# Expert blocks of mixed width in a mixture-of-experts step: 34 blocks a pass in place of 40, every block's rows placed by a 0/1 product

## The chip, the cores and the metric

One core of a Trainium2 chip runs the kernel alone. The time is device microseconds (us) of one execution, the median of the runs taken. Engines are named as in the profile: PE multiplies matrices, DVE is VectorE, ACT is ScalarE, POOL is GpSimd, SP issues most DMAs. The inputs are fixed; all of them are float32.

## What is computed

One inference step for 128 context tokens and 256 latent tokens of width 1024: adaLN modulation, a mixer (neighbourhood attention beside a gated recurrence), a mixture of experts (MoE), a final RMSNorm. The change is in the MoE, for all 384 tokens `t`:

```
s = sigmoid(t @ w_router); sb = s + b_router
# 8 groups of 8 experts: the 4 groups with the best top-2 sum stay; among them the top 8 experts of sb
wk = s[idx] / sum(s[idx]) * 2.5
gates = zeros(n, 64) with wk at idx
act = silu(t @ w_gate_e) * (t @ w_up_e) * gates        # per expert, width 256
routed = act @ w_down_e ; shared = (silu(t @ w_gate_s) * (t @ w_up_s)) @ w_down_s
x += gate_ffn * (routed + shared)
```

Each token uses 8 of 64 experts: 3,072 pairs of token and expert. An expert's weights are three matrices of 1024 KB: gate and up (together "gu") and down ("dn").

## The kernel before

The first third of the execution computes the mixer. Then the router's choice is turned into tables: experts are sorted by load, and each gets a place in a sequence of **blocks** of 128 rows. A block of kind H holds up to 128 tokens of one expert; a block of kind L holds up to 64 tokens of one expert in rows 0 to 63 and up to 64 of another in rows 64 to 127. Blocks come in 4 groups of 16 experts and 10 blocks (4 H and 6 L): `ORDER0, ORDER = "HHHHLLLLLL", "HLLHLHLLHL"`, so a pass over all experts has 40 blocks. If an expert has more tokens than its places hold, a further pass over all groups follows; with these inputs there is none. The first group is written out, the two in the middle are a loop, the last is written out again. Which experts the first four H blocks use is fixed, so that their weights can be loaded before the routing is known.

For one block at turn `u` PE does, in this order (`block_turn` of PE): `gate_up(u)` (the weights of gate and up stream against the block's tokens; for an L block the two experts use two column tiles of 64 and run side by side), `turn_tokens(u+1)` (transposes of the next block's gathered tokens), `down(u-1)`, two transposes of the activation, `block_rows(u+3)` (a small product that yields token numbers and gates of a later block), and where the block before is *placed*, `place(u-1)`.

A block's output rows reach their tokens in one of two ways. **Scattered**: ACT evicts them, scaled by their gates, into `y_sb`, and POOL adds them to a buffer in HBM (`y_dram`, zeroed earlier) with an indirect DMA that accumulates (`scatter`). **Placed**: ACT writes a rounded high part, DVE the rest (`place_low`), DVE makes a 0/1 matrix from the token numbers (`place_matrix`), PE multiplies the two by it (12 products into six banks, `place`), and DVE adds the six banks to `ffn_acc` in SBUF (`place_sums`). 17 blocks are placed (the last two of them in `place_ending`), 23 scattered. At the end `y_dram` is read back (six loads of 512 KB on SP), added, and everything is gated into `x_sb`.

Weights live in a ring of 5 slots, each with a gu and a dn buffer. SP issues, in program order and with waits, for turn `u` the gu loads of block `u` as soon as `gate_up` has released the slot, and behind them the dn loads of block `u-1`. The gather of a block's tokens (`xg <- h2_dram`, indirect DMA on POOL) is issued two blocks ahead. DVE does per turn: `act_sb`, half of the token copy, the placing work, `a_t`, `numbers` (reductions to `slot_val`, `slot_gate`, `slot_tok`, `slot_row`), `select` (the one-hot for the block four ahead), in turns 2 to 7 of the first group `later_passes` (copies of the tables for further passes, made whether they are needed or not), the shared expert's sums in turns 5 to 7, and last `place_sums`. PE's next `gate_up` waits for the first of these sums, for that frees its bank. The shared expert's down product runs inside turns 5 to 7 of the first group, and the product that spreads `gate_ffn` over the partitions (`spread`, L1189) in turn 4.

Of the kernel before, what the change touches and what calls it, by code (L numbers as in the profile page):

```python
# [13 lines left out]
P = 128  # L14
# [20 lines left out]
ORDER0, ORDER = "HHHHLLLLLL", "HLLHLHLLHL"  # L35
NGRP, EPG, BPG = 4, 16, 10
NPASS_BLK = NGRP * BPG
MAXPASS = 4
# [3 lines left out]
NBLK = NPASS_BLK * MAXPASS  # L42
NSIDE = 2 * NPASS_BLK
FIXED = 4
PLACED = (0, 2, 4, 5, 7)
SCATTERED = BPG - len(PLACED)
FIRST_PLACED = (BPG - 3, BPG - 2)
ENDING = (0, 2, BPG - 3, BPG - 2, BPG - 1)
HEAVY = 16
EMPTY = 1024  # L50
MARK = 4096.0
TABLES = 3 + 7
RC = 387
LAT0 = 131
NTAB = NBLK + 4
# [11 lines left out]
def hybrid_step(nc, x_prompt, x_sample, cache_k, cache_v, state_f, state_b, c, c_ctx,  # L67
# [5 lines left out]
    with ctx:  # L73
        KB = 1024
        arena = ctx.enter_context(nc.sbuf_tensor("arena", [P, 207 * 256 + 160], F32))
# [124 lines left out]
        shared_dn = at("shared_dn", [P, 2048], EX + 48)  # L200
# [4 lines left out]
        shared_sb = at("shared_sb", [P, D], EX + 56)  # L205
        x_t = at("x_t", [P, KD * CAP], EX + 108)
        zeros = at("zeros", [P, D], EX + 108)
        a_sh = at("a_sh", [P, TT, 2 * CAP], EX + 112)
        y_sb = [at(f"y_sb{i}", [P, D], EX + 116 + 4 * i) for i in range(2)]
# [31 lines left out]
        shift = little("shift", [P, 2, NSIDE])  # L241
        row_off = little("row_off", [P, 1])
        slot_row = little("slot_row", [P, UN], I32)
# [13 lines left out]
        seq_rank = little("seq_rank", [NE, NE])  # L257
        side_pick = little("side_pick", [NE, NSIDE])
        seq_pick = little("seq_pick", [NE, NE])
        inv_cap = little("inv_cap", [P, NSIDE])  # L260
        fill = little("fill", [P, NSIDE])
        place[0] = EX + 162.5
        limit[0] = EX + 163.5
        seq_expert = little("seq_expert", [1, MAXPASS * NE], I32)


        ffn = [at(f"ffn{t}", [P, D], EX + 4 * t) for t in range(TT)]
        ffn_b = [at(f"ffn_b{t}", [P, D], EX + 12 + 4 * t) for t in range(TT)]
# [3 lines left out]
        y_r = [at(f"y_r{i}", [P, D], EX + 116 + 4 * i, F32R) for i in range(2)]  # L272
        y_hi = [y_r[0], at("y_hi", [P, D], EX + 36, F32R)]
        y_lo_end = at("y_lo_end", [P, D], 12, F32R)
        y_lo = [at(f"y_lo{i}", [P, D], EX + 44 - 4 * i, F32R) for i in range(2)]
# [5 lines left out]

        y_dram = nc.dram_tensor("y_dram", (2 * NTOK, D), F32, kind="Internal").ap()

# [30 lines left out]
        for n, (kind, i) in enumerate(chunks):  # L314
# [3 lines left out]
        S = {n: sem(n) for n in """added cond_loaded vec_loaded cache_loaded bias_loaded block_loaded  # L318
# [10 lines left out]
            gates_made sides_mm sides_evac picks_made sorted_mm gu_used dn_used b_zero  # L329
            sh_mm sh_silu sh_act sh_at_mm sh_at shd_mm shd_evac shared_loaded early_mm  # L330
# [25 lines left out]
        def experts_of(order):  # L356

            n, blocks = 0, []
            for kind in order:
                blocks.append(tuple(range(n, n + 1 + (kind == "L"))))  # L360
                n += len(blocks[-1])
            assert n == EPG
            return blocks
# [3 lines left out]
        def shared_turn(u, first):  # L367

            return (u - FIRST_SHARED,) if first and FIRST_SHARED <= u < FIRST_SHARED + TT else ()

        def shared_outs(u):

            return bank[2 + (u + 1) % 2], bank[2 + u % 2]

        FIRST_SHARED = 5
        SHARED_BANK = (2, 3, 5)
        SPREAD_TURN = 4
# [5 lines left out]

        first_half = (("router_loaded", 16), ("shared_loaded", 48), ("bias_loaded", 32))

        def heavy_places(order):
            return [x[0] for x, kind in zip(experts_of(order), order) if kind == "H"]

        FIRST_FOUR = heavy_places(ORDER0)


        SLOT0 = [x % RING for x in range(EPG)]
        heavy_slot, light_slots = 3, (1, 2, 4, 0)
        SLOT, lights = [], 0
        for x in range(EPG):
            if x in heavy_places(ORDER):
                SLOT.append(heavy_slot)
            else:
                SLOT.append(light_slots[lights % 4])
                lights += 1  # L400
# [20 lines left out]
        assert not {SLOT[x] for x in turns[False][-1]} & {1, 2}  # L421
        assert [SLOT0[x] for x in turns[False][-1]] == [SLOT[x] for x in turns[False][-1]]

        assert max(PLACED) < UN - 2

        assert {SLOT[x] for x in turns[False][UN - 3]} == {1, 2}
        assert not {SLOT[x] for u in (UN - 2, UN - 1) for x in turns[False][u]} & {1, 2}

        def placed_in(last):
            return ENDING if last else PLACED  # L430

        def is_placed(u, first, last=False):
            return u in FIRST_PLACED if first else u % UN in placed_in(last and u >= 0)

        def first_scatters(u):

            return 16 * sum(v not in FIRST_PLACED for v in range(u))

        def scatters_ahead(b, u, last=False):

            back = 1 if u < 0 else 0
            here = placed_in(last and not back)
            return b * (16 * SCATTERED) + 16 * (len(PLACED) - len(FIRST_PLACED) - SCATTERED * back + sum(v not in here for v in range(u % UN)))

        def places_ahead(b, v, each, last=False, first=False):

            if first:
                return each * FIRST_PLACED.index(v)
# [371 lines left out]
        def _(act):  # L820
# [241 lines left out]
            def shared_out(t, outs):  # L1062
                if t:
                    act.wait_ge(S["x2_ready"], t)
# [1220 lines left out]
```

## Time and profile before

| | us |
|---|---|
| median of 3 runs | 927.61 |
| lowest, highest | 926.42, 934.16 |
| span of the profiled execution | 925.6 |

The profile is of one execution. Its span is from the first to the last instruction. Busy time of PE is modelled at the ends of pipelined matmuls, so the distance from the start of one group of matmuls to the next says more than the busy share. `L1538` is line 1538 of the kernel. A matmul in float32 shows as two instructions. "DMA share" is the busy share of the core's 16 DMA engines.

### The profile page before, as it was taken

How to read it: one execution, taken by the hardware profiler on the slowest of the kernel's cores; microseconds unless marked ns; L12 is line 12 of the kernel's file. 1: busy time of each engine (PE TensorE's matmuls, PEld its weight loads, DVE VectorE, ACT ScalarE, POOL GpSimd, SP SyncE). 2: the span in 40 equal slices, each digit the busy share in tenths (PEclk: the TensorE clock that was granted, in tenths of full speed). 3: DMA queues.
4: the chain of work that ended last, by engine and by line, in shares of the span. 5: the costliest groups of instructions: out<-in, count | busy, mean ns of one | idle time of the engine just before them, and what ended most of it. 6: DMA issues, size and time to landing. Idle time of an engine off the chain costs nothing.

```text
span 925.6 us, 12174 instructions
## 1 busy us (share of the span) xinstructions
PE 876.7 (95%) x4185; PEld 513.0 (55%) x4185; DVE 436.2 (47%) x961; ACT 254.9 (28%) x417; POOL 138.6 (15%) x224
## 2 busy tenths in 40 slices
PE   4799999999999899999999999999999999999991
PEld 2387876899998765443344444444444444444440
DVE  1562493677666554233253442542344442433386
ACT  2536634444423431212211122122112112212211
POOL 7410000000002131122110111011111012012202
PEclk9799999999999999999999999999999999999996
DMA  9974885722237398899999999999999999999971
GB/s 353 350 266 172 302 292 211 159 92 65 79 131 267 138 417 310 271 348 406 379 404 420 404 401 402 421 391 406 409 408 409 421 394 408 411 407 400 404 319 68
DMA packets 82416, 294.24 MB, mean 318 GB/s; under 512 B 16876, under 2 KB 33320, under 8 KB 57408
## 3 DMA queue, kind: packets, MB, share of 16 engines
q1 hardware_dynamic: 62352, 263.21, 71.7%
q0 software_dynamic: 11312, 25.85, 9.4%
q10 hardware_dynamic: 8704, 4.54, 1.9%
q8 instruction: 30, 0.49, 0.2%
q14 instruction: 18, 0.15, 0.0%
HBM read 286.11 MB, written 20.71 MB: 332 GB/s over the span
## 4 chain that ended last, share of the span: by engine, by line
PE 75%; DMA 14%; DVE 4%; issue 3%; ACT 1%; SPq 0%; ACTq 0%; POOL 0%; DVEq 0%; POOLq 0%
PE bank L1538 26%; PE bank L1557 13%; PE bank L1150 8%; PE bank L1152 7%; PE bank L1151 7%; DMA y_dram<-y_sb,slot_row 5%; PE bank L1526 4%; DMA chunk_raw<-in_w_ada_dram 3%; DMA b_t<-in_b_ada_dram 2%; PE bank L1178 1%; DMA h_dram<-h_row 1%; DMA dn<-in_w_down_e_dram 1%; PE bank L1230 1%; PE bank L1452 1%; DMA xg<-h_dram,slot_tok 1%
## 5 line engine op out<-in xcount | busy, mean ns | idle before, releaser
L1538 PE MATMUL bank<-gu,x_t 128*64 128x512 f32 (+1 forms) x1024 | 283.8, 596 | 2.6 <-DVE ffn_acc L2247 1.8
L1538 PEld LDWEIGHTS bank<-gu,x_t 128*64 128x64 f32 (+1 forms) x1024 | 101.3, 150 | 160.7 <-issue 157.4
L1557 PE MATMUL bank<-dn,a_t 128*64 128x512 f32 (+1 forms) x512 | 145.4, 597 | 0.6 <-DMA dn<-in_w_down_e_dram 0.6
L2113 DVE TENSOR_TENSOR act_sb<-silu_sb,bank 128x256 f32<-128x256 f32 x40 | 16.8, 421 | 194.8 <-ACT silu_sb L1111 194.8
L1111 ACT ACTIVATE silu_sb<-bank 128x256 f32<-128x256 f32 x40 | 15.4, 385 | 316.1 <-PE bank L1538 316.1
L1557 PEld LDWEIGHTS bank<-dn,a_t 128*64 128x64 f32 (+1 forms) x512 | 48.5, 150 | 69.8 <-issue 68.8
L1150 PE MATMUL bank<-h_hi,chunk_lo 128*128 128x384 f32 x240 | 84.2, 351 | 0.0
L1152 PE MATMUL bank<-h_hi,chunk_hi 128*128 128x384 f32 x240 | 80.6, 336 | 0.0
L1151 PE MATMUL bank<-h_lo,chunk_hi 128*128 128x384 f32 x240 | 80.4, 335 | 0.0
L792 POOL DMA_INDIRECT y_dram<-y_sb,slot_row x23 | 38.5, 1674 | 259.7 <-DVE slot_row L1996 225.7
L780 POOL DMA_INDIRECT xg<-h_dram,slot_tok x40 | 41.5, 1037 | 197.5 <-DVE slot_row L1996 175.5
L475 DVE TENSOR_TENSOR chunk_lo<-chunk_raw,chunk_hi 128x2048 fp32r<-128x2048 f32 x25 | 57.1, 2287 | 15.8 <-ACT chunk_hi L469 15.7
L469 ACT ACTIVATE chunk_hi<-chunk_raw 128x2048 fp32r<-128x2048 f32 x25 | 47.7, 1914 | 42.5 <-PE bank L1152 42.3
L2129 DVE COPY a_t<-bank 128x256 f32<-128x256 f32 x40 | 16.9, 423 | 76.8 <-PE bank L1666 76.6
L1526 PEld LDWEIGHTS bank<-ident,xg 128*128 128x128 f32 x320 | 35.5, 140 | 27.3 <-issue 26.6
L1150 PEld LDWEIGHTS bank<-h_hi,chunk_lo 128*128 128x128 f32 x240 | 45.0, 188 | 7.1 <-issue 5.4
L2247 DVE TENSOR_TENSOR ffn_acc<-ffn_acc,bank 128x512 f32<-128x512 f32 x78 | 47.8, 683 | 0.4
L1576 PE MATMUL bank<-y_r,place_r 128*128 128x512 f32 x174 | 45.1, 401 | 1.2 <-DVE a_t L2129 1.1
L1094 ACT ACTIVATE y_sb<-bank,slot_gate 128x512 f32<-128x512 f32 x46 | 31.6, 687 | 51.9 <-PE bank L1557 50.6
L1151 PEld LDWEIGHTS bank<-h_lo,chunk_hi 128*128 128x128 f32 x240 | 45.1, 188 | 0.3
L1152 PEld LDWEIGHTS bank<-h_hi,chunk_hi 128*128 128x128 f32 x240 | 45.1, 188 | 0.0
L1526 PE MATMUL bank<-ident,xg 128*128 128x128 f32 x320 | 42.8, 277 | 0.6 <-DMA xg<-h_dram,slot_tok 0.6
(366 smaller groups left out, 1099.9 us busy)
## 6 DMA issues: line engine op xcount, KB each, us to landing
gu<-in_w_gate_e_dram SPq DMA_DIRECT2D x64, 1024.0 KB, 14.7
gu<-in_w_up_e_dram SPq DMA_DIRECT2D x64, 1024.0 KB, 18.1
dn<-in_w_down_e_dram SPq DMA_DIRECT2D x64, 1024.0 KB, 19.5
chunk_raw<-in_w_ada_dram SPq DMA_DIRECT2D x24, 1024.0 KB, 8.8
chunk_raw<-in_w_in_dram SPq DMA_DIRECT2D x18, 1024.0 KB, 5.4
chunk_raw<-in_w_out_dram SPq DMA_DIRECT2D x4, 1024.0 KB, 5.1
y_dram<-zeros POOLq DMA_DIRECT2D x1, 3072.0 KB, 18.6
chunk_raw<-in_w_pa_dram SPq DMA_DIRECT2D x2, 1024.0 KB, 5.1
```

Source lines behind the costliest of these rows:

```text
L469: act.activation(chunk_hi[j % HIGHS][:, :], chunk_raw[slot[n]][:, :], ACT.Copy).then_inc(S["chunk_high"], 1)
L475: dve.tensor_tensor(chunk_lo[slot[n]][:, :], chunk_raw[slot[n]][:, :], chunk_hi[j % HIGHS][:, :].bitcast(F32), ALU.subtract).then_inc(S["c ...
L780: pool.indirect_dma_start(xg[u % 2][:, :], None, h2_dram[:, :], bass.IndirectOffsetOnAxis(ap=slot_tok[:, u % UN:u % UN + 1], axis=0), boun ...
L792: pool.indirect_dma_start(y_dram[:, :], bass.IndirectOffsetOnAxis(ap=slot_row[:, u % UN:u % UN + 1], axis=0), y_sb[u % 2][:, :], None, bou ...
L1150: pe.matmul(out, left[1], right[0], start=start, stop=False)
L1151: pe.matmul(out, left[0], right[1], start=False, stop=False)
L1152: return pe.matmul(out, left[0], right[0], start=False, stop=stop)
L1526: mm = pe.transpose(bank[k // 4][:, (k % 4) * P:(k % 4 + 1) * P], xg[u % 2][:, k * P:(k + 1) * P], ident[:, :])
L1538: mm = pe.matmul(bank[2 + u % 2][at_x, :].rearrange("p (g n) -> p g n", g=2), x_t[:, cols], wide[:, :, k, :], start=(k == 0), stop=(k == K ...
L1557: mm = pe.matmul(outs[half][at_x, :], a_t[:, cols], dn[slot_of(x, first)][:, wc], start=(k == 0), stop=(k == 1))
L1576: return pe.matmul(out[:, :], place_r[:, t * P:(t + 1) * P], y[:, halves[half]], start=start, stop=not start)
L2247: dve.tensor_tensor(ffn_acc[t][:, cols], ffn_acc[t][:, cols], out[:, :], ALU.add).then_inc(S["place_out"], 1)
```

## The change

- A third kind of block, **M**: 96 rows of one expert and 32 of another. PE's tiles are then four column tiles of 32 (`tiles_of`): three with the same weights and one with the other expert's, so 4 matmuls for each k in place of 2 (L) or 1 (H).
- The first group has the blocks "MMMHHLHLHL" (10), the three others "MLLMLLML" (8): 34 blocks. Per pass 12 experts may have up to 96 tokens, 12 up to 32, 4 up to 128, 36 up to 64.
- Nothing is scattered. `y_dram`, its zeroing, `slot_row`, and the loads at the end are gone; `place` follows every block. `y_hi` and `y_lo` are single buffers. At the last turn DVE gates `ffn_acc` into `x_sb` (`sums_in`, six operations) ahead of its other work.
- The shared expert's down product runs before block 0 and starts `ffn_acc` by an ACT copy; its weights come with its gate and up weights, ahead of the MoE. `spread` moves to turn 0.
- Three experts, not four, are loaded before the routing is known; `passes_ready` comes earlier. Slot 4 of the ring holds the shared weights first, also for its dn buffer.
- `later_passes` keeps its place in DVE's turn (turns 2 to 8 of the first group); it has fewer small copies. `select` for an M block is two operations. Tables are made for up to 5 passes, not 4.

The diff, cut to its core:

```diff
-ORDER0, ORDER = "HHHHLLLLLL", "HLLHLHLLHL"
-NGRP, EPG, BPG = 4, 16, 10
+WIDE, NARROW = 96, 32
+ORDER0, ORDER = "MMMHHLHLHL", "MLLMLLML"
+NGRP, EPG, BPG0, BPG = 4, 16, len(ORDER0), len(ORDER)
...
+        def tiles_of(x, u, first):
+            if kind_of(u, first) == "H":
+                return [slice(0, P)]
+            second = x != turns[first][u][0]
+            if kind_of(u, first) == "L":
+                return [slice(HALF * second, HALF * second + HALF)]
+            return [slice(q * QW, q * QW + QW) for q in ((3,) if second else (0, 1, 2))]
...
+        SLOT0 = [(0, 3, 1, 4, 2)[x % RING] for x in range(EPG)]
+        often, others = 1, (3, 4, 2, 0)
+        SLOT = [often if x % 4 == 0 else others[(x - x // 4 - 1) % 4] for x in range(EPG)]
...
-            pool.dma_start(y_dram.rearrange("(t p) d -> p t d", p=P), zeros[:, :].unsqueeze(1).to_broadcast([P, 2 * TT, D])
...
                 for k in range(KD):
                     for x in experts:
-                        at_x = rows_of(x, experts)
...
+                        for at_x in tiles_of(x, u, first):
+                            cols = slice(k * CAP + at_x.start, k * CAP + at_x.stop)
+                            mm = pe.matmul(bank[2 + u % 2][at_x, :].rearrange("p (g n) -> p g n", g=2), x_t[:, cols], wide[:, :, k, :],
+                                           start=(k == 0), stop=(k == KD - 1))
...
-                    if u and is_placed(u - 1, first, last) and not (last and u == UN - 1):
-                        place(u - 1, b, last, first)
+                    if not (first and u == 0) and not (last and u == BPG - 1):
+                        place(i - 1, u)
...
+            pe.wait_ge(S["shared_dn_loaded"], 16)
+            shared_down(0)
+            shared_turn_act(2)
+            shared_down(1)
+            shared_down(2)
             block_turn(0, True)
...
-                dve.tensor_scalar(slot_row[:, u:u + 1], slot_val[:, u:u + 1], row_off[:, 0:1], None, ALU.add).then_inc(S["idx_ready"], 1)
...
                     if first:
                         later_passes(u)
...
-                    elif placing:
-                        place_sums(u - 1, b, last, first)
+                    if placing and not ending:
+                        place_sums(i - 1, u)
```

## Rows read from the trace of the kernel before

**Rows 1.** The page, part 2: DMA share of each fortieth of the span, tenths

```profile
DMA  9974885722237398899999999999999999999971
```

**Rows 2.** The chain that ended last, 700 to 770 us: start, length, what

```profile
700.17 6.97 PE bank L1538 x16
...
715.11 7.09 PE bank L1538 x32
...
757.17 7.09 PE bank L1538 x32
...
769.00 6.97 PE bank L1538 x16
```

**Rows 3.** Stages: length, then PE, PEld, DVE, ACT, POOL (xcount), clock, DMA share, GB/s

```profile
660.00:700.00 40.00, 39.79 (x175) 17.57 (x175) 15.77 (x36) 6.46 (x12) 4.72 (x4) 1.00 1.02 413
...
586.00:604.00 18.00, 17.75 (x85) 8.54 (x83) 9.02 (x20) 3.27 (x6) 0.99 (x1) 1.00 1.02 421
606.00:616.00 10.00, 10.00 (x39) 4.76 (x37) 2.47 (x9) 1.85 (x4) 2.71 (x2) 1.00 0.98 365
722.00:734.00 12.00, 11.79 (x55) 6.23 (x55) 8.08 (x18) 2.36 (x4) 1.00 (x1) 1.00 1.01 420
```

**Rows 4.** Timeline of the last block and the end

```profile
853.91 0.33 SPq L545 DMA_DIRECT2D gu<-in_w_gate_e_dram  x1
...
885.07 7.09 PE L1538 MATMUL bank<-gu,x_t 128*64 128x512 f32 x32
...
899.55 3.65 PE L1557 MATMUL bank<-dn,a_t 128*64 128x512 f32 x16 [0.62 <-DMA dn<-in_w_down_e_dram]
...
904.67 1.22 DVE L2180 TENSOR_TENSOR ffn<-ffn,ffn_b 128x1024 f32<-128x1024 f32 x1
```

**Rows 5.** DMA issues at 853 to 857 us: size, median us to landing

```profile
gu<-in_w_up_e_dram SPq DMA_DIRECT2D x2, 1024.0 KB, 27.1
```

**Rows 6.** PE's timeline: start and length; first two blocks, the spread product

```profile
360.67 7.11 PE L1538 MATMUL bank<-gu,x_t 128*128 128x512 f32 x16
...
369.71 7.11 PE L1538 MATMUL bank<-gu,x_t 128*128 128x512 f32 x16 [0.30 <-ACT x_t L1083]
...
416.85 3.67 PE L1189 MATMUL bank<-m_late,pick 128*128 128x512 f32 x8 [0.55 <-DVE a_t L2129]
```

**Rows 7.** The chain again: shared down product; four tiles of 32; router product

```profile
432.64 3.54 PE bank L1452 x8
...
64.77 1.85 PE bank L1178 x16
...
324.49 5.31 PE bank L1413 x48
```

**Rows 8.** Timeline of all engines at the end of one placed turn

```profile
711.96 3.00 PE L1576 MATMUL bank<-y_r,place_r 128*128 128x512 f32 x12
...
713.59 0.20 DVE L1996 TENSOR_SCALAR slot_row<-slot_val,row_off 128x1 int32<-128x1 f32 x1
713.71 0.55 DVE L1981 TENSOR_TENSOR onehot<-rank_of,rank_tab 128x384 bf16<-128x384 f32 x1
714.29 2.48 DVE L2247 TENSOR_TENSOR ffn_acc<-ffn_acc,bank 128x512 f32<-128x512 f32 x4
...
715.11 1.94 PE L1538 MATMUL bank<-gu,x_t 128*64 128x512 f32 x8 [0.16 <-DVE ffn_acc L2247]
```

**Rows 9.** DVE's table copies: timeline of turns 2 to 4, then a line's group

```profile
394.71 2.18 DVE L2073 COPY seq_expert<-seq_expert 1x3 int32<-1x3 int32 x10
...
406.27 2.26 DVE L2080 COPY rank_tab<-rank_tab 128x6 f32<-128x6 f32 x10
...
418.12 2.47 DVE L2080 COPY row_tab<-row_tab 128x24 bf16<-128x24 bf16 x10
...
L2085 DVE COPY row_tab<-row_tab 128x960 bf16<-128x960 bf16 x2 | 0.8, 410 | 0.1
```

**Rows 10.** DMA issues at 375 to 385 us: size, us to landing

```profile
gu<-in_w_gate_e_dram SPq DMA_DIRECT2D x1, 1024.0 KB, 4.9
```

More of the change, by code:

```diff
@@ L420, in hybrid_step @@
             assert earlier(x, False) >= 0 or earlier(x, False) + EPG >= max(y for y in range(EPG) if SLOT0[y] == SLOT[x])
[L421 to L448, printed above, removed]
-            return b * (each * len(PLACED)) + each * (placed_in(last).index(v) + len(FIRST_PLACED) - len(PLACED))
-        def low_rows(v, last):
-            return y_lo_end if last and v == UN - 3 else y_r[1 - v % 2]
+        assert [SLOT0[x] for x in turns[True][-1]] == [SLOT[x] for x in turns[False][-1]]
+        assert ORDER0[-1] == ORDER[-1] and AHEAD % 2 == 0 and UN % 2 == 0
         def place_outs(u):
             return [(0, 0, bank[2 + (u + 1) % 2]), (1, 0, bank[0]), (2, 0, bank[1]), (0, 1, bank[4]), (1, 1, bank[5]), (2, 1, bank[6])]
-        def rows_of(x, order_x):
-            return slice(0, P) if len(order_x) == 1 else slice(HALF * order_x.index(x), HALF * order_x.index(x) + HALF)
         def split_high(act, n):
@@ L805, in block_turn @@
                         count(tok_no[:, :], [[1, NTOK]], 0).then_inc(S["zero_filled"], 1)
-                    if not (first and u == 0) and not (u and is_placed(u - 1, first, last)):
-                        scatter(i - 1, u - 1, first_scatters(u - 1) if first else scatters_ahead(b, u - 1, last))
-            gather(0, 0)
-            gather(1, 1)
+            gather(0, 0, col_of(0, True))
+            gather(1, 1, col_of(1, True))
             pool.wait_ge(S["passes_ready"], 1)
@@ L1125, in _ @@
             shared_silu(2)
+            for n in range(2 * TT):
+                shared_out(n)
             block_turn(0, True)
@@ L1561, in down, with product @@
                                 mm.then_inc(S["dn_half"], 1)
-            def place(v, b, last=False, first=False):
-                i, at_y = b * UN + v, v % 2
-                y_low = low_rows(v, last)
-                ahead = lambda each: places_ahead(b, v, each, last, first)
-                outs = place_outs(v + 1)
-                halves = [slice(0, 512), slice(512, 1024)]
+            halves = [slice(0, 512), slice(512, 1024)]
+            def product(out, at_t, y, half, start=False, stop=False, matrix=place_r):
+                return pe.matmul(out[:, :], matrix[:, at_t * P:(at_t + 1) * P], y[:, halves[half]], start=start, stop=stop)
@@ L1570, in place @@
+            def place(i, u):
+                outs = place_outs(u)
                 pe.wait_ge(S["x_first"], i + 3)
                 pe.wait_ge(S["x_second"], i + 3)
[L1572 to L1580 removed]
+                pe.wait_ge(S["place_made"], i + 1)
+                pe.wait_ge(S["y_half"], i + 1)
+                for t, half, out in outs[0:3]:
+                    product(out, t, y_hi, half, start=True)
@@ L2209, in ending_sums, with place_sums @@
+            def place_sums(i, u):
+                for n, (t, half, out) in enumerate(place_outs(u)):
+                    cols = slice(512 * half, 512 * half + 512)
+                    dve.wait_ge(S["place_mm"], 6 * i + (n + 1))
+                    dve.tensor_tensor(ffn_acc[t][:, cols], ffn_acc[t][:, cols], out[:, :], ALU.add).then_inc(S["place_out"], 1)
+            def ending_sums(i):
+                outs = place_outs(BPG - 1)
                 for t in range(TT):
@@ L2239, in place_sums @@
-            def place_sums(v, b, last=False, first=False):
-                for n, (t, half, out) in enumerate(place_outs(v + 1)):
-                    cols = slice(512 * half, 512 * half + 512)
-                    dve.wait_ge(S["place_mm"], places_ahead(b, v, 6, last, first) + n + 1)
-                    if first and v == FIRST_PLACED[0]:
-                        dve.tensor_copy(ffn_acc[t][:, cols], out[:, :]).then_inc(S["place_out"], 1)
-                    else:
-                        dve.tensor_tensor(ffn_acc[t][:, cols], ffn_acc[t][:, cols], out[:, :], ALU.add).then_inc(S["place_out"], 1)
@@ L2249, in _ @@
-            numbers(2, 2)
+            numbers(2, 2, True)
             shared_a(2)
```

691 lines of the change are left out of this document (297 added, 394 removed).

## The prediction

> **What bounds the kernel now.** I read the page's 40 slices first: from the tenth or so of the MoE to its end the DMA engines are full [rows 1]. The chain of waits is next: it runs through PE, and the distance between two `gate_up` says what a block costs, 14.94 us where the block before it is placed (700.17 to 715.11) and 11.83 where it is scattered (757.17 to 769.00) [rows 2]. The stages show both at once: over 40 us PE is busy for 39.79 and the DMA share is 1.02 at 413 GB/s [rows 3]. So PE sets the pace and DMA has almost nothing left. How little shows at the end: the last block's weights are issued from 853.91 and wanted at 885.07 [rows 4], and the DMA view has 27.1 us from issue to landing for their second matrices [rows 5]. A change that makes PE faster meets the DMA a few us later. That is the question of this case.
>
> All sums are made against the profiled span, 925.6. The median, 927.61, is 2.0 above it, and I add that at the end. About 1% is what a measurement of this kernel can tell from no change: 918.3 and 936.9 are the limits.
>
> **Does it stay one pass?** The loads of the experts follow from the reference's inputs; I evaluated its router on them. Experts 0, 1 and 2 get 78, 39 and 85 tokens (limit 96), the next by load 124, 99, 92, 79 (limit 128), then 78 to 64 (96), 63 and fewer (64), and the lowest twelve at most 28 (32). All fit, so 34 blocks and no further pass.
>
> **The start.** Block 0 started at 360.67 [rows 6]. Three shared down products of 3.54 [rows 7] now stand ahead of it, and one pair of transposes (0.4) moves there from turn 0: 360.67 + 10.6 + 0.4 = 371.7. The loads hide beside this: the fourth expert's came after the routing before, and does so still. Turn 0 lasted 369.71 - 360.67 = 9.0, less the 0.4, plus the spread product with its wait, 3.67 + 0.55 [rows 6]: block 1 starts at 384.5. None of this is gained or lost, it stood in turns 4 to 7 before. Two waits are new here. SP waits for the shared down products (371.7) before the dn load of block 1's second expert; behind it stand loads that need block 0's end (378.8) anyway, and that dn is wanted after 400. POOL waits for the same before it counts `tok_no`, and behind that stands a gather that is wanted a turn later.
>
> **An M block.** Its `gate_up` is 64 matmul instructions (8 k, 4 tiles, two instructions each), H has 16 in 7.1 us, L 32 in 7.1. The trace shows four tiles of 32 columns in L1178: 16 instructions in 1.85 us [rows 7], that is four steps of 0.43 and a tail of 0.1, so four tiles run side by side as two do. It bursts only 16 long. For a long stream the router product bounds what PE can take up: 48 instructions with as many weight loads in 5.31 us, 111 ns a pair [rows 7]; M asks for 64 pairs in 7.1, also 111 ns. Lower bound: the same as L. Upper bound by the row: 1.85 per 16, 7.4 in `gate_up` and 3.7 in `down`, 0.4 a block. I take nothing.
>
> **A placed turn.** 14.94. At its end DVE runs `slot_row`, `select`, then the first of six sums, and PE's next `gate_up` waits 0.16 for that sum (0.68 after 714.29) while PE's own products ended, as modelled, at 714.96 [rows 8]. So DVE's chain sets the turn by a hair. Without `slot_row` it is 0.12 shorter (713.59 to 713.71); an M block's `select` is two operations, some 0.1 more. I take 14.85.
>
> **Table copies, the cost hidden in the diff.** `later_passes` stands behind `select` and ahead of `place_sums`. Before, nothing was placed in turns 2 to 7 of the first group, so it ran in DVE's idle time. Now each of those turns ends in sums that PE waits for, and the copies push them back one for one. Ten small copies take 2.18, 2.26, 2.47 and a large one some 0.3 with each [rows 9]. Now: turn 2 keeps its ten, 2.5; turns 3 and 4 have eight, 1.8 + 0.3 and 2.0 + 0.4; turns 5 to 8 have seven larger ones, at 0.41 for tables of 40 blocks [rows 9] some 0.36 with the gap for 32, 2.5. Sum 9.5. It is hidden (0) only if the sums were not what PE waits for; I take all of it. The next group starts at 384.5 + 9 x 14.85 + 9.5 = 527.7.
>
> **PE to the last block.** 23 more turns of 14.85: the last `gate_up` could start at 869.3, against 885.07 before [rows 4]. The count by work agrees: six blocks fewer at 11.83 are 71 off, 17 more placings at 3.0 [rows 8] are 51 on, and 9.5 of copies leave 10 to 16.
>
> **DMA to the last block.** In the last three groups a turn takes two experts, 6.29 MB, and its share of the gathered rows, 0.35 MB (some 2,030 of 3,072 rows of 4 KB in 24 blocks). DMA moves 421 and 420 GB/s where it has work and no scatter falls in, the second for weights alone, and drops to 365 over 10 us around a scatter [rows 3]. At 420.5 a turn needs 15.8 us, PE 14.85. So DMA falls back 0.93 us a turn. The room for it: gu of block u can be issued when block u-2 has ended its `gate_up`, 7.1 into its turn, and is wanted two turns after that turn's start; 29.7 - 7.1 - 10.0 (4.19 MB) - 2.4 (a load lands 4.9 us after its issue, of which 2.5 is moving it [rows 10]) = 10.2. After eleven turns it is gone, and PE waits for weights. In bytes: from 534.8 (block 10 frees its slots and DMA is caught up, for the first group asks for less) until the last gu lands it must move 22 x 4.19 + 21 x 2.10 + 21 x 0.35 = 143.7 MB, 341.7 us, and 2.4 to land: 878.9. What may still be queued at 534.8 is 0 to 2.5 MB, 0 to 6 us; I take 1. The last block starts at 879.9, 5.2 earlier than before, 10.6 later than PE could. Removing 23 scatters is what makes this bound as low as it is: they cost DMA time too.
>
> The Trainium skill's page "DMA: Bandwidth & Descriptors" (Specifications) states a fabric ceiling of 435 GB/s and an HBM limit per core of about 358. By 358 the 143.7 MB would take 401 us, and the change would be 59 us slower than I say; this trace disagrees with that, with 420 and 421. By 435 they would take 330 us and end just before PE does, which is the first rival below.
>
> **The end.** From the last `gate_up` to the end was 40.5. Its down product waited 0.62 for weights behind the reads of `y_dram`, and L2180 with a second gating stood in DVE's last sums [rows 4]. Now no read stands ahead, the three sums are 1.2 shorter; `sums_in` (six operations of about 1.2, 7.4) runs beside the last `gate_up` of 7.1 and makes `act_sb` some 2.8 later, but it is wanted only after `down`, 3.6 further on; I keep 0.3 of the 0.62. 40.5 - 1.5 = 39.0. If `down` does not cover it, it costs up to 2.
>
> Sum: 879.9 + 39.0 = 918.9, and 2.0: **921**. Costed at nothing: POOL's clearing of `xg` and its new tables (POOL waits for the stored rows then), the earlier count of passes on DVE (before the gather may start anyway), the zeroing of `y_dram` that is gone (PE had work throughout).
>
> **The rivals.**
> 1. *PE sets the end, weights keep up.* For: PE never waited for gu, the landing has room of 10 us. Against: 6.64 MB in 14.85 us is 447 GB/s, which no row shows. 869.3 + 41.0 = **910**. Chance 0.22.
> 2. *The copies are hidden* (DVE has more slack than it seems). Then all starts 9.5 earlier and DMA bounds: **911.5**. Against: the 0.16 wait. 0.12; with rival 1 too **901**, 0.05.
> 3. *Slower: M blocks don't run four tiles at full rate.* Each us on an M block costs 12. PE has 10.6 to spare against DMA, so nothing shows up to 0.9 a block apart from the first group's three; it is slower by over 1% from 2.2 us a block (869.3 + 12 x 2.2 + 41.0 = 937). At a quarter more, 1.8 + 0.9, it is **943**. For: only bursts of 16 were seen. Against: in them a step of four takes what a step of H takes (7.1 / 16 = 0.44). 0.10. The Trainium skill's page "TensorE: Matmul & The Clock Gate" (Part 3, measured speedup) gives 2.38 for three column tiles of 32, not 3, which is that quarter; the rows here show full overlap.
> 4. *It doesn't do what it says*: loads that don't fit add 32 blocks, over 450 us. Ruled out by the loads above, under 0.01.
>
> The rest, 0.03, is a stall I don't see.
>
> **How the numbers follow.** DMA's bound with the copies exposed has 0.47. Its own range is 915 to 928. At 413 GB/s, the row with scatters in it, the 143.7 MB take 6 us more, the queue at 534.8 may add up to 5; M's 0.4 a block and turns of 14.94 hide under DMA but for 2 us in the first group; it is up to 5 less if those experts whose slots come free a turn earlier give DMA more room. The tail of it under 918.3 is 0.03. Faster by over 1%: 0.22 + 0.12 + 0.05 + 0.03 = 0.42. Slower: 0.09 of rivals 3 and 4. Within 1%: 0.49. The range 908 to 932 leaves out the 901 case, most of rival 3 and the unseen.
>
> **What would show it.** Start of block 0 at 371 to 372. First group's turns 2, 3 and 4 at 17 and above, PE waiting for `ffn_acc`; turns 1 and 9 at 14.9. M's `gate_up` 7.1 (64 instructions). In the last two groups turns of 15.8 with PE waiting for gu, the DMA at 420. No scatter, no wait for y_dram. The prediction is wrong if turns there stay at 14.9, or if L1538 takes over 8 us for M.

## The result and the profile after

| | before | after |
|---|---|---|
| median of 20 runs, us | 931.15 | 926.55 |
| lowest, highest | 926.23, 934.83 | 921.23, 928.34 |
| span of the profiled execution | 925.6 | 924.8 |

The ratio is 0.995, with a 95% interval of 0.993 to 0.997: the changed kernel is faster by half a per cent, 4.6 us, and that is within the 1% that I had called "same". I had said 921; it is 5.5 more, inside the range. Beside the 927.61 of the three runs shown then, 921 was a saving of 6.6; beside the 931.15 of twenty runs it would be one of 10.2, and 4.6 were measured.

Two executions stand far off, one of 1010.98 us in experiment 2 (mean clock 0.842) and one of 2781.08 us of the kernel before beside experiments 1 to 3, and no reading rests on them.

The times lie in two groups, which the mean granted clock of each execution tells apart. After: 6 of 20 at a clock of 0.984 or more, 921.2 to 925.5 (median 922.7), and 14 under it, 926.0 to 928.3 (927.8). Of the twenty executions of before in the table only the times are on record; of twenty others, beside experiments 1 to 3, 9 have a clock of 0.984 or more, 925.2 to 929.2 us (median 926.9), and 11 one of 0.982 or less, 931.0 to 934.9 (934.0). The profile of before is of the first kind (925.6), the one of after of the second. So the two spans, 0.8 apart, don't compare like with like. That has to be taken out before anything else is read.

The stretches just ahead of the router show it. Columns as in [rows 3]: length, PE, PEld, DVE, ACT, POOL, then clock, DMA share, GB/s. Before:

```profile
320.00:325.00 5.00, 2.82 (x23) 2.63 (x23) 4.77 (x13) 4.41 (x12) 3.22 (x28) 1.00 0.86 298
325.00:330.00 5.00, 5.00 (x47) 5.00 (x47) 0.83 (x3) 1.20 (x4) 4.82 (x5) 1.00 1.02 428
```

After:

```profile
320.00:325.00 5.00, 3.89 (x22) 3.70 (x22) 4.53 (x13) 3.98 (x13) 4.11 (x35) 0.68 1.03 433
325.00:330.00 5.00, 5.00 (x25) 5.00 (x25) 0.00 (x0) 0.76 (x3) 4.94 (x5) 0.50 1.00 416
330.00:335.00 5.00, 5.00 (x26) 5.00 (x26) 0.15 (x1) 0.33 (x1) 3.78 (x3) 0.50 1.00 421
335.00:340.00 5.00, 5.00 (x23) 3.84 (x23) 4.58 (x44) 3.48 (x6) 0.00 (x0) 0.61 1.02 423
```

From 322 to 339 TensorE was granted 1.2 GHz in place of 2.4. PE's timeline of after shows the price: the router's 48 instructions took 10.34 us, where they had taken 5.47 (5.31 in [rows 7]), and the transposes behind them 5.22 (before 3.9, with short waits in it).

```profile
322.24 1.97 PE L1334 MATMUL bank<-ident,xhat 128*128 128x128 f32 x8 [1.11 <-DVE xhat L1619]
324.00 10.34 PE L1341 MATMUL bank<-w_router_sb,h_t 128*128 128x64 f32 x48
334.14 5.22 PE L1357 MATMUL bank<-ident,h_t 128*128 128x128 f32 x24
```

PE's waits ahead of it are the same in both: 1.30 and 1.11 us for `xhat` (before 1.29 and 1.12).

Block 0 started at 376.2, not at 371.7. Now the page of after, part 2, second half of the strips:

```profile
PEclk9999999999999969999999999999999999999997
DMA  9984875722237294689697689999999999999961
GB/s 353 348 288 173 303 278 205 159 92 82 78 115 263 75 401 177 252 353 399 245 378 302 250 347 419 419 420 420 420 420 422 419 421 420 419 418 421 421 284 68
```

There are no scatters left, and 280.8 MB are moved in place of 294.2. From slice 24 on (555 us) to the last blocks the DMA moves 418 to 422 GB/s without a break. PE's timeline has the starts of `gate_up` (start, length, then the wait ahead of it and what ended it):

```profile
376.18 7.07 PE L1467 MATMUL bank<-gu,x_t 128*32 128x512 f32 x64
...
421.76 7.10 PE L1467 MATMUL bank<-gu,x_t 128*128 128x512 f32 x16 [2.48 <-DVE ffn_acc L2107]
...
455.57 4.94 PE L1467 MATMUL bank<-gu,x_t 128*64 128x512 f32 x22 [2.21 <-issue]
...
533.23 7.07 PE L1467 MATMUL bank<-gu,x_t 128*32 128x512 f32 x64 [0.39 <-DVE ffn_acc L2107]
...
593.89 7.09 PE L1467 MATMUL bank<-gu,x_t 128*64 128x512 f32 x32 [0.22 <-DVE ffn_acc L2107]
...
730.92 7.09 PE L1467 MATMUL bank<-gu,x_t 128*64 128x512 f32 x32 [0.28 <-DVE ffn_acc L2107]
...
746.18 7.07 PE L1467 MATMUL bank<-gu,x_t 128*32 128x512 f32 x64 [0.22 <-DMA gu<-in_w_up_e_dram]
...
777.73 7.07 PE L1467 MATMUL bank<-gu,x_t 128*32 128x512 f32 x64 [0.72 <-DMA gu<-in_w_up_e_dram]
...
873.40 7.08 PE L1467 MATMUL bank<-gu,x_t 128*32 128x512 f32 x64 [0.54 <-DMA gu<-in_w_up_e_dram]
...
888.39 7.09 PE L1467 MATMUL bank<-gu,x_t 128*64 128x512 f32 x32
```

Three regimes are to be seen. In turns 2 to 4 of the first group PE waits over 2 us, twice by name for `ffn_acc`, that is for DVE (the row at 455.57 names no releaser; experiment 1 takes all three waits away), and turns take 17.5, 17.0 and 16.8. From block 10 (533.23) to block 23 (730.92) a turn takes 197.69 / 13 = 15.2 us, and the waits are at most 0.4. From block 24 (746.18) PE waits for gu in most turns, and a turn takes 15.8 (142.21 / 9). The stages show the same from the side of the DMA (last two columns):

```profile
531.00:540.00 9.00, 8.62 (x73) 3.24 (x71) 4.88 (x13) 0.00 (x0) 0.99 (x1) 1.00 0.79 329
540.00:550.00 10.00, 9.99 (x53) 5.08 (x51) 6.70 (x16) 2.36 (x4) 0.99 (x1) 1.00 0.85 334
550.00:600.00 50.00, 49.49 (x291) 21.54 (x289) 25.07 (x55) 7.07 (x12) 2.98 (x3) 1.00 1.01 419
600.00:700.00 100.00, 98.96 (x597) 44.61 (x593) 52.41 (x117) 16.51 (x28) 6.12 (x7) 1.00 1.02 420
700.00:800.00 100.00, 97.08 (x600) 42.87 (x598) 51.02 (x110) 14.14 (x24) 6.78 (x7) 1.00 1.01 420
800.00:860.00 60.00, 55.73 (x339) 25.65 (x337) 31.26 (x68) 9.44 (x16) 3.97 (x4) 1.00 1.01 420
```

From 600 to 700 PE is busy for 99.0 of 100 us, in the next hundred for 97.1, and then for 55.7 of 60, while the DMA stays at 420. The stage from 540 to 550 is no steady one: its first 2.5 us are nearly empty, and from about 542.5 on the DMA is full (the DMA view under "Weights" below).

### The profile page after: what moved, and what is told of

The parts are those of the page before. It is cut to its first block, busy times and chain, and to the rows that moved or that the text cites. A ratio compares the mean times of both kernels' runs of the same rounds, so it can differ in the third digit from the quotient of the medians.

```text
span 924.8 us, 13517 instructions
## 1 busy us (share of the span) xinstructions
PE 864.5 (93%) x4887; PEld 514.4 (56%) x4887; DVE 490.0 (53%) x1019; ACT 241.0 (26%) x393; POOL 94.3 (10%) x206
## 4 chain that ended last, share of the span: by engine, by line
PE 73%; DMA 17%; DVE 5%; issue 2%; SPq 1%; ACT 1%; POOL 1%; ACTq 0%; DVEq 0%; POOLq 0%
PE bank L1467 21%; DMA gu<-in_w_up_e_dram 12%; PE bank L1486 9%; PE bank L1078 8%; PE bank L1080 7%; PE bank L1079 7%; PE bank L1495 4%; DMA chunk_raw<-in_w_ada_dram 3%; PE bank L1455 3%; PE bank L1363 2%; DMA b_t<-in_b_ada_dram 2%; PE bank L1106 1%; PE bank L1158 1%; PE bank L1382 1%; PE bank L1341 1%
## 5 line engine op out<-in xcount | busy, mean ns | idle before, releaser
L1467 PE MATMUL bank<-gu,x_t 128*32 128x512 f32 (+2 forms) x1408 | 240.9, 594 | 19.9 <-DVE ffn_acc L2107 9.6
L1467 PEld LDWEIGHTS bank<-gu,x_t 128*32 128x32 f32 (+2 forms) x1408 | 82.1, 124 | 163.7 <-issue 155.9
L1486 PE MATMUL bank<-dn,a_t 128*32 128x512 f32 (+2 forms) x704 | 123.8, 596 | 0.0
L2107 DVE TENSOR_TENSOR ffn_acc<-ffn_acc,bank 128x512 f32<-128x512 f32 x192 | 117.7, 682 | 1.5 <-PE bank L1495 0.5
L2049 DVE TENSOR_TENSOR act_sb<-silu_sb,bank 128x256 f32<-128x256 f32 x34 | 14.3, 421 | 179.4 <-ACT silu_sb L1043 179.4
L2099 DVE SCALAR_TENSOR_TENSOR y_lo<-bank,slot_gate,y_hi 128x512 fp32r<-128x512 f32 x68 | 50.9, 748 | 55.8 <-ACT y_hi L1033 55.5
L1486 PEld LDWEIGHTS bank<-dn,a_t 128*32 128x32 f32 (+2 forms) x704 | 36.1, 124 | 64.0 <-issue 64.0
L1033 ACT ACTIVATE y_hi<-bank,slot_gate 128x512 fp32r<-128x512 f32 x68 | 46.8, 688 | 82.4 <-PE bank L1486 82.4
L434 DVE TENSOR_TENSOR chunk_lo<-chunk_raw,chunk_hi 128x2048 fp32r<-128x2048 f32 x25 | 57.1, 2287 | 15.8 <-ACT chunk_hi L428 15.7
L1495 PE MATMUL bank<-y_hi,place_r 128*128 128x512 f32 x198 | 65.0, 408 | 0.0
L1495 PE MATMUL bank<-y_lo,place_r 128*128 128x512 f32 x198 | 61.4, 391 | 0.0
L1495 PEld LDWEIGHTS bank<-y_lo,place_r 128*128 128x128 f32 x198 | 37.1, 188 | 6.5
```

The source lines that it names most:

```text
L434: dve.tensor_tensor(chunk_lo[slot[n]][:, :], chunk_raw[slot[n]][:, :], chunk_hi[j % HIGHS][:, :].bitcast(F32), ALU.subtract).then_inc(S["c ...
L1033: act.activation(y_hi[:, half * 512:half * 512 + 512], bank[outs[half]][:, :], ACT.Copy, scale=slot_gate[:, col:col + 1]).then_inc(S["y_re ...
L1467: mm = pe.matmul(bank[2 + u % 2][at_x, :].rearrange("p (g n) -> p g n", g=2), x_t[:, cols], wide[:, :, k, :], start=(k == 0), stop=(k == K ...
L1486: mm = pe.matmul(outs[half][at_x, :], a_t[:, cols], dn[slot_of(x, first)][:, wc], start=(k == 0), stop=(k == 1))
L1495: return pe.matmul(out[:, :], matrix[:, at_t * P:(at_t + 1) * P], y[:, halves[half]], start=start, stop=stop)
L2099: dve.scalar_tensor_tensor(y_lo[:, cols], bank[outs[half]][:, :], slot_gate[:, col:col + 1], y_hi[:, cols].bitcast(F32), ALU.mult, ALU.sub ...
```

## Experiments

The ratios and medians are against the kernel before, which ran beside each set (931.84 in the median for experiments 1 to 3, or 931.4 without the one of 2781.08; 931.51 for 4 to 7). Where an output is not the reference's, the text that stands ahead of the run says so.

### 1. The table copies off PE's path

```diff
-                    if first:
-                        later_passes(u)
                     if placing and not ending:
                         place_sums(i - 1, u)
+                    if first:
+                        later_passes(u)
```

> The changed kernel with its table copies (later_passes) moved behind place_sums in the first group, so that they run on DVE while PE does the next gate_up. Theory (copies exposed one for one, then DMA sets the end): turns 2 to 8 of the first group shrink from 15.3 to 17.5 us to about 15.2, block 10 starts 9.5 us earlier than the changed kernel's 533.2 (523.7), DMA becomes full about 9 us earlier than its 550, and the whole is 8.5 to 9.5 us shorter: about 917 beside 926.6. Rival 1 (the copies were hidden): turns 2 to 8 and the time stay, 926.6. Rival 2 (DMA was full already, in some queue that the byte rates don't show, so that what PE gains in the first group it gives back waiting for weights): block 10 starts 9.5 earlier, but the last block no more than 0 to 4 earlier, 923 to 926.

Measured: 917.19 (914.04 to 918.40), ratio 0.986 (0.982 to 0.990), 9.4 less than the changed kernel. Some of that is the share of executions whose clock fell (here 3 of 6, there 14 of 20); the two profiles, both with the fall, have spans of 915.9 and 924.8, 8.9 apart. PE's timeline (blocks 3, 10 and 33):

```profile
419.01 7.10 PE L1467 MATMUL bank<-gu,x_t 128*128 128x512 f32 x16 [0.17 <-issue]
...
524.11 6.21 PE L1467 MATMUL bank<-gu,x_t 128*32 128x512 f32 x56 [0.35 <-DVE ffn_acc L2107]
...
879.44 7.09 PE L1467 MATMUL bank<-gu,x_t 128*64 128x512 f32 x32
```

and its stages:

```profile
530.00:540.00 10.00, 9.97 (x57) 4.91 (x51) 5.83 (x14) 2.36 (x4) 0.99 (x1) 1.00 0.75 293
540.00:550.00 10.00, 10.00 (x66) 3.66 (x66) 3.62 (x8) 1.67 (x3) 0.00 (x0) 1.00 1.02 424
```

The wait at block 3 is 0.17 in place of 2.48. From block 0 to block 10 it took 524.11 - 375.78 = 148.3 us, against 533.23 - 376.18 = 157.1: 8.7 less. The last block started 8.95 earlier, and its DMA is full from about 533.5, not from 542.5 (the first stage holds the empty start, as the one from 540 to 550 did). So the copies were paid nearly one for one, and the gain came through to the end whole although weights set the end: the DMA had been waiting for slots, and got them earlier. Rival 2 of this run (weights take it back) is out.

### 2. The fall of the clock ahead of the router

```diff
             def turn_rows2(t):
+                if t:
+                    pe.wait_ge(S["out_done"], 3)
+                    for n in range(10 - t):
+                        pe.transpose(bank[2][:, 0:P], ident[:, :], ident[:, :])
                 pe.wait_ge(S["xhat2"], t + 1)
```

In the changed kernel:

> The changed kernel with nine and eight extra transposes of the identity (0.13 us each) in the two gaps of 1.30 and 1.11 us in which PE waits for xhat2 just ahead of the router; nothing of them is used. Theory (PE's activity drops there far enough in some executions that the granted clock falls to the 1.2 GHz level for some 15 us, router 10.1 us in place of 5.3, and all that follows is 4.5 us late): with the gaps filled every execution keeps 1.00 there, and all times lie at 921 to 923.5, median 4 to 5 us under the changed kernel's 926.6. Rival (the fall has another cause, the filler doesn't touch it): times in two groups as before, median 926 to 927. What it could cost if the filler delays the transposes: 0.1 us.

Measured: 922.61, ratio 0.991 (0.988 to 0.994); nine of the ten lie at 919.85 to 923.42, with a median of 922.25. The same in the kernel before:

> The kernel before with the same filler in the same two gaps (1.29 and 1.12 us there). Theory (the two groups of times, 926 to 929 and 930 to 935, are the same fall of the clock, which has nothing to do with the change): all times at 926 to 929, median 927.5, ratio to the unfilled kernel 0.995 to 0.997; the change is then worth the same 5.5 us with and without the fall. Rival (the fall has another cause): two groups again, ratio 1.000.

Measured: 928.42 (926.07 to 930.44), ratio 0.998 (0.995 to 1.000). The stages of the two, changed kernel first:

```profile
320.00:325.00 5.00, 4.45 (x38) 3.98 (x37) 4.73 (x11) 3.72 (x10) 2.91 (x17) 1.00 0.79 244
325.00:330.00 5.00, 5.00 (x48) 5.00 (x46) 1.73 (x6) 1.73 (x5) 4.72 (x22) 1.00 0.96 390
```
```profile
320.00:325.00 5.00, 4.75 (x43) 4.51 (x42) 4.08 (x12) 4.31 (x13) 4.61 (x30) 1.00 1.00 418
325.00:330.00 5.00, 4.75 (x43) 4.44 (x43) 1.17 (x13) 1.42 (x3) 4.94 (x5) 1.00 1.03 434
```

PE's timeline of experiment 3, which has the same filler, shows the stretch (the second transposes and the router):

```profile
321.10 1.16 PE L1338 MATMUL bank<-ident,xhat 128*128 128x128 f32 x8 [0.23 <-DVE xhat L1623]
322.10 5.47 PE L1345 MATMUL bank<-w_router_sb,h_t 128*128 128x64 f32 x48
```

With the gaps filled the second group of times is gone in both kernels; the lowest mean clock of any of these executions but the one of 1010.98 us is 0.985, where 11 of 20 of the unfilled kernel before were at 0.982 or less. So filling these two gaps removes the fall. It is not part of the change, and it strikes by chance: the waits were as long (1.29 and 1.12, 1.30 and 1.11) in the profile whose clock held and in the one where it fell. From the start of the second transposes to block 0 it is 376.18 - 322.24 = 53.9 us with the fall and 48.4 to 48.6 in experiments 2 to 4, which are filled: the fall costs 5.4.

Like against like the change is worth 928.42 - 922.25 = 6.2 us with the gaps filled, and 926.9 - 922.7 = 4.2 between the unfilled executions whose clock held. In the kernel before the filler gains less than I expected, and the interval reaches 1.000: its median is 1.5 us above those 926.9. What the filler costs there was not looked into, and it is most of the distance from 4.2 to 6.2.

### 3. Both edits together

> The changed kernel with both edits, the copies behind place_sums and the filler. Theory: the two gains add, since one lies before the first block and the other between blocks 2 and 10 and DMA is waiting for slots through both: 926.6 - 9.2 - 4.5 = 913, ratio to the kernel before 0.98. Rival (DMA full already): 918 to 921.

Measured: 912.22 (910.36 to 914.30), ratio 0.982 (0.978 to 0.986). The gains add: 926.55 - 912.22 = 14.3, and 9.4 + 4.3 = 13.7 apart (4.3 is 926.55 - 922.25). This kernel computes what the reference does and is 1.8% faster than before and 1.5% than the changed one. Experiments 4, 5 and 7 are made from it, since its times scatter little; experiment 6 is made from the changed kernel with the gaps filled and the copies where they were.

### 4. Fewer bytes in the last three groups

```diff
-                sp.dma_start(dn[k][:, :], w_down_e[0, e].rearrange(...)).then_inc(dn_ready[k], 16)
+                n = 2 * D if group is None else D
+                sp.dma_start(dn[k][:, 0:n], w_down_e[0, e].rearrange(...)[:, 0:n]).then_inc(dn_ready[k], 16)
```

> The kernel with copies behind and gaps filled (912.2 us), loading in groups 1 to 3 only the first half of each expert's down matrix (0.52 of 1.05 MB; the products read what lies in the other half, so the output is not the reference's). A turn of these groups then moves 5.6 MB, 13.3 us at 420 GB/s, under PE's 15.2. Theory (weights set the pace from block 24 on, 15.8 a turn): no wait for gu is left, turns 24 to 33 are 15.2 (mean of the thirteen turns before: 15.2), the last gate_up starts at 518.2 + 23 x 15.2 = 867.8 in place of 873.5, and the time is 906.5. Rival 1 (the 15.8 come from something else on PE or DVE): 912. Rival 2 (as the prediction had it, a turn bound by PE alone takes 14.85): 898 to 899.

Measured: 907.12 (906.24 to 908.34), 5.1 less than 912.22 (expected 5.7). PE's timeline at the end:

```profile
839.06 7.09 PE L1472 MATMUL bank<-gu,x_t 128*64 128x512 f32 x32
...
854.06 7.07 PE L1472 MATMUL bank<-gu,x_t 128*32 128x512 f32 x64
...
869.03 3.23 PE L1472 MATMUL bank<-gu,x_t 128*64 128x512 f32 x14
```

No wait for gu is left, turns stay at 15.0 to 15.4 to the end, and the DMA is down to 365 to 373 GB/s. So the weights were the bound from block 24 on, and they cost 5 us. It was not 13 (rival 2 here): a turn bound by PE and DVE takes 15.2, not the 14.85 of the prediction.

### 5. What an M block costs

```diff
-            return [slice(q * QW, q * QW + QW) for q in ((3,) if second else (0, 1, 2))]
+            return [slice(HALF * second, HALF * second + HALF)]
```

> The same kernel (912.2 us) with the twelve M blocks' products tiled as in L blocks, two tiles of 64 columns in place of four of 32, so 32 instructions in gate_up in place of 64 (rows 64 to 95 get the other expert's weights: the output is not the reference's). Theory (an M block costs PE what an L block costs): gate_up stays 7.07 to 7.10, turns and time stay, 912. Rival (M blocks cost PE some tenths each, 0.1 to 0.4): block 10 starts 0.3 to 1.2 earlier than 518.2, and M turns in groups 1 and 2 are shorter by that.

Measured: 912.24 (911.57 to 912.73), against 912.22. From block 0 to block 10 it is 520.59 - 372.18 = 148.4 us, and with M blocks 148.5. M's `gate_up` takes 7.07 with 64 instructions and 7.09 with 32. An M block costs PE nothing over an L block.

### 6. All blocks placed, but still forty

```diff
-ORDER0, ORDER = "MMMHHLHLHL", "MLLMLLML"
+ORDER0, ORDER = "HHHHLLLLLL", "HLLHLHLLHL"
...
-                ins = pool.memset(limits[:, pas - 1:pas], pas - 1 + 0.004)
+                ins = pool.memset(limits[:, pas - 1:pas], 1000.0 + pas)
```

> One part of the change alone: every block placed by products and none scattered, but in the old 40 blocks a pass (HHHHLLLLLL, then HLLHLHLLHL three times), with the gaps filled and the copies where the change has them. Sides hold experts in plain order whatever their loads, rows over a side's 64 are left out, and one pass is forced, so the output is not the reference's. To compare: 922.6 for the changed kernel with the gaps filled. Theory (each block costs a placed turn of 14.9 to 15.2, weights are no bound at 5.4 MB a turn, 358 GB/s): 372.5 + 12.9 + 38 x 15.05 + 8.5 of copies + 36.5 + 1.8 = 1004. So placing alone makes the kernel some 76 slower and six blocks fewer bring 82 back. Rival (what the scatters and the readings of y_dram cost beside PE was more than the placings): under 960.

Measured: 1002.55 (1001.40 to 1003.33), ratio 1.077 (1.073 to 1.081). PE's timeline near the end, and a stage:

```profile
918.37 7.09 PE L1455 MATMUL bank<-gu,x_t 128*64 128x512 f32 x32
...
933.01 7.09 PE L1455 MATMUL bank<-gu,x_t 128*64 128x512 f32 x32
...
947.92 7.03 PE L1455 MATMUL bank<-gu,x_t 128*128 128x512 f32 x16
...
600.00:700.00 100.00, 98.82 (x418) 47.89 (x416) 53.38 (x115) 14.43 (x25) 6.92 (x7) 1.00 0.84 335
```

Turns in the loop are 14.95 to 15.15, and the DMA is at 335. This is the change taken apart: placing everything, with all else that the change moves (the exposed copies, the shared product ahead of block 0, no reading of `y_dram`), costs 1002.6 - 928.4 = 74 us against the filled kernel before, and six blocks fewer give 1002.6 - 922.3 = 80 back. The small net of the change is the difference of two large terms. The M blocks are what pays; the placing of all blocks, with the exposed copies in it, eats nine tenths of that.

### 7. A faster turn on PE, with weights as they are

```diff
-                    if not last or u + 4 < BPG:
-                        select(i + 4, u + 4, first)
                     if placing and not ending:
                         place_sums(i - 1, u)
+                    if not last or u + 4 < BPG:
+                        select(i + 4, u + 4, first)
```

> The kernel with copies behind and gaps filled (912.2 us) with select moved behind place_sums too, in every turn. PE waits 0.16 to 0.32 for the first sum in most turns while its own products ended; select is 0.56 to 0.63 of DVE ahead of that sum. Expected on PE: turns of groups 0 to 2 fall from 15.2 to about 14.9, block 10 starts 2.5 to 3 earlier than 518.2. Theory (DMA bytes set the end): DMA becomes full 3 us earlier, the first wait for weights comes some turns earlier than block 24, and the end gains 2.5 to 3.5 in all: 909. Rival (PE sets the end): 0.3 in each of 33 turns, 9 in all, 903. Second rival (DMA is bound already so that nothing is gained): 912.

Measured: 910.28 (909.21 to 911.40), ratio 0.978 (0.975 to 0.981). PE's timeline, blocks 10, 19 to 21, and 33:

```profile
517.76 7.07 PE L1471 MATMUL bank<-gu,x_t 128*32 128x512 f32 x64
...
652.49 7.09 PE L1471 MATMUL bank<-gu,x_t 128*64 128x512 f32 x32
...
667.67 7.09 PE L1471 MATMUL bank<-gu,x_t 128*64 128x512 f32 x32 [0.16 <-DMA gu<-in_w_up_e_dram]
...
683.50 7.08 PE L1471 MATMUL bank<-gu,x_t 128*32 128x512 f32 x64 [0.78 <-DVE ffn_acc L2111]
...
873.18 7.09 PE L1471 MATMUL bank<-gu,x_t 128*64 128x512 f32 x32
```

Turns bound by PE fall to 14.95, and from block 0 to block 10 it takes 145.4 in place of 148.5. But the first wait for gu comes at block 20, four earlier than before, and turns are 15.8 from there: from block 0 to block 33 it takes 873.18 - 372.40 = 500.8, against 873.48 - 369.72 = 503.8 without the edit. Of the 0.3 a turn, which over 33 turns would be 8 to 9, 3.0 come through: at block 20 it was 5.2 ahead (295.3 against 300.4 from block 0), and from there it waits for weights four turns longer than the other. What is left is what it had won by block 10 (3.1), where the DMA became full. In the median it is 1.9. It is the fastest of the kernels here that compute what the reference does.

## Why the prediction was right or wrong

**The sum.** In the units of the profiled execution I had 918.9 and it was 924.8, 5.9 more. The parts: 4.5 is the clock ahead of the router, 1.0 the turns up to block 10, 3.0 the DMA from block 10 on, and the end is 2.6 shorter than I said. By mechanism the forecast was right (weights set the end; copies exposed; M free), and what failed is a term put at nothing without a reason: the clock ahead of the router. Beside executions whose clock held (922.7) the 921 is 1.7 too low, and that it is so near is partly luck: the 2.6 by which the end was too long take back most of the 4.0 by which turns and weights were too short.

**The start.** This is the step that failed: "All sums are made against the profiled span, 925.6. The median, 927.61, is 2.0 above it". Three runs of before were shown, 926.42, 927.61 and 934.16, and I took the spread for noise. The span and the lower two belong to the group with the full clock. So the sum was that of an execution without the fall, on the side of before as of after, and the 2.0 that I added for the median is little more than what any execution has over its span (926.56 beside 924.8 is 1.8). What the runs showed in its place: the clock fell in 11 of 20 executions of before and in 14 of 20 of after, at 7.1 and 5.1 us each, so that the median of before was 931.15 and not 927.61, and block 0 of the profiled after came 4.5 late: 5.6 for the fall (53.9 in place of the 48.4 that the prediction has from the second transposes at 323.34 to 371.7), less the 1.1 by which PE reached those transposes earlier. Where the clock held, the changed kernel takes 922.7 in the median, and I had said 921. With the gaps filled block 0 starts at 372.67, 369.72, 371.17, 372.18 and 372.40 in experiments 2 to 5 and 7, on either side of the 371.7 predicted (the second transposes themselves start at 321.1 to 324.2 there). The rest of this step stood: turn 0 was 12.9 (12.8 predicted).

**M blocks.** Right: 7.07 to 7.10 for 64 instructions, 3.64 for the 32 of `down`. Rival 3 is refuted twice, by the timeline and by experiment 5. The bursts of 16 [rows 7] did speak for a stream of 64.

**A placed turn.** Wrong by 0.35: 15.2 in the loop, not 14.85. I had measured the turn on one distance, 700.17 to 715.11 [rows 2], and read it from the chain, which lists that `gate_up` only from 700.17 on. PE's timeline has its start at 700.03, so that turn took 15.08, and the scattered one 11.69, not 11.83. And it was a kind of turn that the loop of the changed kernel, all M and L, doesn't have: an H block behind an L block. The trace of before has L blocks behind L blocks at 15.2 to 15.3, on PE's timeline:

```profile
467.42 7.09 PE L1538 MATMUL bank<-gu,x_t 128*64 128x512 f32 x32
...
482.70 7.09 PE L1538 MATMUL bank<-gu,x_t 128*64 128x512 f32 x32 [0.24 <-issue]
...
497.90 2.41 PE L1538 MATMUL bank<-gu,x_t 128*128 128x512 f32 x5
...
700.03 7.11 PE L1538 MATMUL bank<-gu,x_t 128*128 128x512 f32 x16
```

An H block's turn behind another H is shorter: 14.83 for turn 4 of experiment 1. In experiment 6 an L block behind an H takes 14.95, an H behind an L 15.05, an L behind an L 15.15. Two distances more would have told. In the result it hardly shows: nine turns at 15.05 (experiment 1) are 1.8 more by block 10, the copies 0.8 less, and 1.0 is left, since weights set the pace behind it. It also moved the point where weights begin to bind: at 0.6 a turn (15.8 less 15.2) they did at block 24, after 14 turns and 8.4 us, where I had said eleven turns at 0.93, block 21. In experiment 7, at 0.85 a turn, it took ten turns, 8.5 us. So the room is 8.4 to 8.5 and not the 10.2 of the prediction.

**Table copies.** Right in kind, 0.8 too high: 9.5 predicted; block 10 is 8.7 nearer to block 0 without them, and the time 9.4 shorter. This was the cost that the diff hides best, as it doesn't touch the line: the change moved other work behind it.

**Weights.** Right in kind: 15.8 a turn from block 24 to 33 (15.8 predicted), at 420 GB/s. Late by 3.0. I let the DMA be full from the moment block 10 frees its slots, with 1 us still queued. That moment was 540.3. SP's waits between 525 and 552 show that SP had nothing else to issue until then: it waited 14.6 us for the `gate_up` that frees the slot (queue and line, what it waited for, us, times, longest):

```profile
SPq L505 <- PE bank L1467: 26.1, 2, 14.6
```

And the DMA view of that stretch, in fortieths of 27 us, shows that nothing was queued: the DMA engines stood empty from 538.5 to 541.2, and the full rate came at 542.5.

```profile
DMA  0094999999999999999300009399999999999999
GB/s 0 0 182 182 461 413 437 401 413 473 413 437 400 425 461 413 437 388 364 109 24 6 0 0 146 109 437 400 437 437 400 437 425 437 437 413 425 449 400 419
```

The loads went out at 540.55. At 334 GB/s, the ten us from 540 to 550 did the work of 7.9, so the full stretch in effect began at 542.1, 0.8 later than 540.3 + 1. The rest of the 3.0 is bytes: from 540 to the landing of the last gu some 144.4 MB were moved, by the stages' rates up to the start of block 33 and less 1.0 MB for the 2.4 us of landing, where I had counted 143.7; that is 1.7 us, and 420.0 for 420.5 GB/s is 0.4. Of what the 0.7 MB consist was not traced.

The Trainium skill's page "HBM Reference" (Specifications (TRN2)) says that a core which streams alone measures about 425 GB/s, above the share of 358 that I had cited from the Trainium skill's page "DMA: Bandwidth & Descriptors". The traces agree with it nearly: 420 to 421 here, over 300 us.

**The end.** 36.4 against 39.0 predicted and 40.5 before. What I had named is there: from the last `gate_up` to the end of DVE's last operation it took 32.4, before 34.1, so 1.7 less, and I had 1.5. `sums_in` did delay `act_sb` (it starts 10.4 after the last `gate_up`, before 7.7, so 2.7 later; predicted 2.8), and `down` covered it but for the 0.23 us that PE waited. The other 2.5 lie behind DVE's last operation: 4.0 from there to the end, before 6.5. No step of mine touched this. It is not chance: all eight profiles of the changed kernel and what was made from it have 3.9 to 4.5 there, and the two of the kernel before, plain and with the filler, 6.5. Nor is it the moving of the output: in the profile of before the DMA is quiet from 921.3 on, 4.3 before the end, in that of after from 923.4, 1.4 before it. What part of the change shortens it stays open.

**The chances.** The case that I thought likeliest came (weights bind, copies exposed). Rival 1 (weights keep up) fell with the waits for gu and with experiment 4, rival 2 (copies hidden) with experiment 1, rival 3 with experiment 5; there was one pass, so rival 4 too. None of them had the clock. "Same" had 0.49, and the interval of 0.993 to 0.997 is in it.

## What to carry to other kernels

When a kernel's few runs lie in two groups close to a per cent apart, look at the granted clock of each before a profile is taken as the baseline: here one profile fell in either group, and 4.5 of the 5.9 us by which the sum missed were that. When work is moved into turns that used to have idle time, price all that already sits in that time; here copies that the diff left in their place took about 9 us, twice the whole gain, and moving them by two lines gave it back. And where a second resource is a few per cent behind the first, work a faster turn through to the end by that resource's own clock: of the 8 to 9 us that a faster turn could have given, 3 arrived.

## What the runs showed of the hardware

- Behind over 40 us of unbroken matmuls and two waits of 1.3 and 1.1 us within 5 us, the granted clock fell to the 1.2 GHz level, for some 17 us in the profile. By the mean clocks that was so in 11 of 20 executions of before and 14 of 20 of after. With seventeen transposes that nobody uses in the waits it was so in none of 47 executions (mean clock 0.985 and up), leaving out the one of 1010.98 us.
- The clock can fall at a wait for weights as well: in experiments 1 to 3 `gate_up` of block 30 took 8.78 us in place of 7.1, behind a wait of 1.9 to 2.1. The granted clock was 0.81 from 835 to 840 us in experiment 1. After the same wait (2.05) it held in the changed kernel, at 1.00. The fall cost nothing there, since weights were the bound: block 33 started no later against block 10 (355.3 us in experiments 1 and 3) than in the changed kernel (355.2). Experiment 1:

```profile
832.80 8.78 PE L1467 MATMUL bank<-gu,x_t 128*64 128x512 f32 x32 [1.95 <-DMA gu<-in_w_up_e_dram]
```

- The fall ahead of the router costs the kernel before more than the changed one: 926.9 and 934.0 are the medians of its two groups beside experiments 1 to 3, 7.1 apart, where after has 922.7 and 927.8, 5.1 apart. Why it is more there stays open.
- Four column tiles of 32 rows run side by side for 64 instructions at the full rate of two tiles of 64 or one of 128: 7.07, 7.09 and 7.11 us.
